# First feed-forward projection of a two-block transformer kernel, with the weights stationary in TensorE and the 256 tokens moving

## The reference, cut to what matters

```python
h = _rmsnorm(x, g_pre_ffn[l]) * (1.0 + sc2) + sh2
f = jnp.square(jax.nn.relu(h @ w_ff1[l])) @ w_ff2[l]
x = x + gt2 * _rmsnorm(f, g_post_ffn[l])
```

## Time and profile before

| | |
|---|---|
| median of 3 runs | 1873.92 us |
| runs | 1872.31 to 1875.08 us |
| span of the profiled execution, first to last instruction | 1870.4 us |
| device time of the profiled execution | not listed apart from the span; the median lies 3.5 us above the span |
| PE busy, share of the span | 1826.9 us, 98% |
| weight loads (PEld) busy | 1495.8 us, 80% |
| DVE busy | 1297.3 us, 69% |
| ACT busy | 901.1 us, 48% |

### The profile page before, as it was taken

The page is one execution under the profiler, slowest core; times in us unless marked ns, Lnnn a source line. Parts: engine busy times, 40 slices in busy tenths (PEclk is TensorE's granted clock), DMA queues, the critical chain, the costliest instruction groups (busy, mean ns, idle before and its releaser), DMA issues.

```text
span 1870.4 us, 25828 instructions
## 1 busy us (share of the span) xinstructions
PE 1826.9 (98%) x8418; PEld 1495.8 (80%) x8418; DVE 1297.3 (69%) x1700; ACT 901.1 (48%) x1272; POOL 181.8 (10%) x268
## 2 busy tenths in 40 slices
PE   8999999989999999999999998999999999999998
PEld 6777777778688888888888886888888888888886
DVE  5777787885798677686776888666666664545545
ACT  6555565453444544544444455444444444444443
POOL 1212211210000000031000130000000010000000
PEclk9999999989999999999999999999999999999999
DMA  7767776836486686688888874877777755555553
GB/s 253 259 223 250 231 237 227 282 117 213 129 266 220 200 277 212 215 302 284 279 281 283 300 260 147 259 231 236 229 233 229 236 195 194 192 193 193 195 192 136
DMA packets 180029, 424.90 MB, mean 227 GB/s; under 512 B 15376, under 2 KB 15616, under 8 KB 179584
## 3 DMA queue, kind: packets, MB, share of 16 engines
q1 hardware_dynamic: 151376, 320.07, 52.0%
q0 software_dynamic: 28304, 103.89, 17.7%
q10 hardware_dynamic: 288, 0.16, 0.1%
HBM read 421.97 MB, written 2.10 MB: 227 GB/s over the span
## 4 chain that ended last, share of the span: by engine, by line
PE 84%; DVE 7%; DMA 5%; issue 3%; ACT 2%; DVEq 0%; POOL 0%; ACTq 0%; POOLq 0%
PE bank L1723 26%; PE bank L1725 26%; PE bank L1724 26%; DMA ada_raw<-in_w_ada 4%; DVE w_lo L1086 2%; PE bank L1779 2%; DVE acc_a L1096 1%; PE bank L1853 1%; PE bank L1852 1%; DVE acc_b L1096 1%; PE bank L1871 1%; DVE y L1224 1%; DMA raw<-in_w_in_a 0%; PE bank L1863 0%; DVE y L1254 0%
## 5 line engine op out<-in xcount | busy, mean ns | idle before, releaser
L1086 DVE TENSOR_TENSOR w_lo<-raw,w_hi 128x1024 fp32r<-128x1024 f32 (+1 forms) x608 | 741.7, 1225 | 420.8 <-ACT w_hi L609 419.5
L609 ACT ACTIVATE w_hi<-raw 128x1024 fp32r<-128x1024 f32 (+1 forms) x608 | 637.0, 1050 | 743.9 <-PE bank L1725 684.2
L1723 PE MATMUL bank<-w_hi,h_hi 128*128 128x512 f32 (+1 forms) x2304 | 910.4, 395 | 11.5 <-DVE h_lo L1187 5.4
L1725 PE MATMUL bank<-w_hi,h_lo 128*128 128x512 f32 (+1 forms) x2304 | 898.4, 390 | 0.0
L1724 PE MATMUL bank<-w_lo,h_hi 128*128 128x512 f32 (+1 forms) x2304 | 897.2, 389 | 0.0
L1723 PEld LDWEIGHTS bank<-w_hi,h_hi 128*128 128x128 f32 x2304 | 434.8, 189 | 105.1 <-DVE w_lo L1086 6.0
L1725 PEld LDWEIGHTS bank<-w_hi,h_lo 128*128 128x128 f32 x2304 | 434.6, 189 | 91.6
L1724 PEld LDWEIGHTS bank<-w_lo,h_hi 128*128 128x128 f32 x2304 | 435.2, 189 | 85.9
L508 POOL DMA_DIRECT2D ada_raw<-in_w_ada x192 | 103.0, 537 | 1123.7 <-DVE acc_a L1096 867.0
L1096 DVE SCALAR_TENSOR_TENSOR acc_a<-ada_raw,cond,acc_a 128x1024 f32<-128x1024 f32 x128 | 164.4, 1284 | 31.2 <-DMA ada_raw<-in_w_ada 30.9
L1096 DVE SCALAR_TENSOR_TENSOR acc_b<-ada_raw,cond,acc_b 128x1024 f32<-128x1024 f32 x64 | 85.3, 1333 | 12.1 <-DMA ada_raw<-in_w_ada 12.0
(11 more groups left out here) (183 smaller groups left out, 1028.3 us busy)
## 6 DMA issues: line engine op xcount, KB each, us to landing
raw<-in_w_ff SPq DMA_DIRECT2D x256, 512.0 KB, 4.4
ada_raw<-in_w_ada POOLq DMA_DIRECT2D x192, 512.0 KB, 4.8
raw<-in_w_in SPq DMA_DIRECT2D x176, 512.0 KB, 4.5
raw<-in_w_in_a SPq DMA_DIRECT2D x72, 512.0 KB, 4.6
raw<-in_w_out_a SPq DMA_DIRECT2D x32, 512.0 KB, 4.7
raw<-in_w_o SPq DMA_DIRECT2D x32, 512.0 KB, 4.7
raw<-in_w_moba SPq DMA_DIRECT2D x16, 512.0 KB, 4.6
raw<-in_w_dsa SPq DMA_DIRECT2D x16, 512.0 KB, 4.8
```

The costliest lines, as they stand in the source:

```text
L609: act.activation(used(w_hi, turn, s), used(raw, turn, s), ACT.Copy).then_inc(hi_ready, 1)
L1086: dve.tensor_tensor(used(w_lo, turn, s), used(raw, turn, s), used(w_hi, turn, s).bitcast(F32), ALU.subtract).then_inc(lo_ready, 1)
L1723: pe.matmul(out_ap, hi, rhs_hi, start=start, stop=False)
L1725: return pe.matmul(out_ap, lo, rhs_hi, start=False, stop=stop)
```

## The change

The projection's matmuls swap their operands. A 128x128 tile of the weights (`w_hi` or `w_lo`) is stationary, and all 256 tokens of a slice of `h_hi` or `h_lo` move. A unit becomes 24 matmuls of 256 columns (2 banks, 2 slices, 2 halves of a bank, 3 products). A PSUM bank now holds two groups of 128 features by 256 tokens side by side. The result has the layout of `f_t`, so DVE's square writes `f_t` itself, and the transposes, their two copies and the semaphores `f_turned` and `f_t_ready` go. ACT's relu waits for the squares of the turn before. `f_tok` is called `f_pos`.

On ScalarE:

```diff
-            def relu(p, c, turn):
-                for t in range(T):
-                    chunk_result(t, turn, c + CHUNK_FF1)
-                    act.wait_ge(f_turned, c * T + t + 1)
-                    act.activation(f_tok[:, t, :], pair[p][t][:, :], ACT.Relu).then_inc(evicted[p][t], 1)
-            def keep_f(c):
-                act.wait_ge(f_turned, c * T + 1 + T)
-                act.activation(f_t[:, bass.ds(c * 4, 4), 0:P], two(banks[TURNED][:, :], 4), ACT.Copy)\
-                    .then_inc(f_t_ready[0], 1)
+            def relu(p, c, turn, first=False):
+                for b in range(T):
+                    chunk_result(b, turn, c + CHUNK_FF1)
+                    if not first:
+                        act.wait_ge(f_sq, c * T + b + 1 - T)
+                    act.activation(f_pos[:, b, :], pair[p][b][:, :], ACT.Relu).then_inc(evicted[p][b], 1)
             def ff1_turn(c):
                 for s in range(UPT):
                     split(c + TURN_FF1, s + AHEAD)
-                    if s == 4:
-                        keep_f(c - 1)
```

On VectorE:

```diff
-            def square(p, use):
-                for t in range(T):
-                    dve.wait_ge(evicted[p][t], use + 1)
-                    dve.tensor_tensor(f_tok[:, t, :], f_tok[:, t, :], f_tok[:, t, :], ALU.mult).then_inc(f_sq, 1)
-            def keep_f(c):
-                dve.wait_ge(f_turned, c * T + 2 + T)
-                dve.tensor_copy(f_t[:, bass.ds(c * 4, 4), P:SEQ], two(banks[OUTS][:, :], 4)).then_inc(f_t_ready[1], 1)
+            def square(p, c, use):
+                for b in range(T):
+                    dve.wait_ge(evicted[p][b], use + 1)
+                    dve.tensor_tensor(f_t[:, bass.ds(c * 4 + 2 * b, 2), :], two(f_pos[:, b, :]), two(f_pos[:, b, :]),
+                                      ALU.mult).then_inc(f_sq, 1)
```

On TensorE:

```diff
-            def turn_f(c):
-                for t in range(T):
-                    pe.wait_ge(f_sq, c * T + t + 1)
-                    turn_rows(f_tok, t, 4, banks[TURNED + t], f_turned)
+            def ff1_unit(turn, s, p, use, h=None):
+                if h is not None:
+                    pe.wait_ge(h_lo_ready, h + s + 1)
+                pe.wait_ge(lo_ready, unit_of(turn, s) + 1)
+                for b in range(T):
+                    if s == 0:
+                        pe.wait_ge(evicted[p][b], use)
+                    for kk in range(KG):
+                        k = KG * s + kk
+                        for half in range(2):
+                            at = kk * CH + (2 * b + half) * P
+                            out_f = pair[p][b][:, half * SEQ:(half + 1) * SEQ]
+                            hi, lo = w_hi[:, s % SLOTS, at:at + P], w_lo[:, s % SLOTS, at:at + P]
+                            pe.matmul(out_f, hi, h_hi[:, k, :], start=s == 0 and kk == 0 and half == 0, stop=False)
+                            pe.matmul(out_f, hi, h_lo[:, k, :], start=False, stop=False)
+                            mm = pe.matmul(out_f, lo, h_hi[:, k, :], start=False,
+                                           stop=s == UPT - 1 and kk == KG - 1 and half == 1)
+                    if s == UPT - 1 and b == 0:
+                        mm.then_inc(front_done, 1)
+                mm.then_inc(mm_done, 1)
             def ff1_turn(c, p, use):
                 for s in range(UPT):
-                    chunk_unit(c + TURN_FF1, s, p, use)
-                    if s == 3:
-                        turn_f(c - 1)
+                    ff1_unit(c + TURN_FF1, s, p, use)
...
-            norm_turn(2, TURN_FF1, PAIR_A, 23, H_NORM2)
+            norm_turn(2, TURN_FF1, PAIR_A, 23, H_NORM2, ff1_unit)
...
             ff2_half(1, 0, 0, start=True)
-            turn_f(15)
             pe.wait_ge(gain_ready, 8)
             ff2_half(0, 1, 0, start=True).then_inc(mm_done, 1)
-            for t in range(T):
-                pe.wait_ge(f_t_ready[t], D_FF // CH)
             ff2_half(1, 1, 0, start=True).then_inc(mm_done, 1)
             ff2_turn(0, 0, 2)
             ff2_turn(1, 1)
```

More of the change, by code:

```diff
@@ L234, in two_block_kernel @@
             f_t = sb("f_t", [P, D_FF // P, SEQ], on=a)
-        f_tok = acc_b[:, 0:T * CH].rearrange("p (t n) -> p t n", t=T)
+        f_pos = acc_b[:, 0:T * CH].rearrange("p (t n) -> p t n", t=T)
         norm_tmp = post_gain[:, 0:2 * KG * SEQ].rearrange("p (b n) -> p b n", b=2)
@@ L352, in two_block_kernel @@
         f_sq = sem("f_sq")
-        f_turned = sem("f_turned")
-        f_t_ready = [sem(f"f_t_ready{t}") for t in range(T)]
         f_hi_ready = sem("f_hi_ready")
@@ L1017, in ff1_turn @@
                     split(c + TURN_FF1, s + AHEAD)
-                    if s == 4:
-                        keep_f(c - 1)
             norm_turn(2, TURN_FF1)
-            relu(PAIR_A, 0, TURN_FF1)
+            relu(PAIR_A, 0, TURN_FF1, first=True)
             with act.Fori(0, 7) as it:
@@ L1054, in ff2_turn @@
                         round_f(c + 1, 1 - b)
-            split(TURN_FF2, AHEAD)
-            keep_f(15)
-            for t in range(T):
-                act.wait_ge(f_t_ready[t], D_FF // CH)
-            for s in range(1, UPT):
+            for s in range(UPT):
                 split(TURN_FF2, s + AHEAD)
                 if s == 4:
+                    act.wait_ge(f_sq, D_FF // CH * T)
                     round_f(1, 1)
@@ L1073, in _ @@
                 act.wait_ge(y_squared, 4 * CHUNKS + n + 1)
-                act.activation(f_tok[:, 0, :], banks[t * CHUNKS + c][:, :], ACT.Square, accum_out=y_sq[:, t, c:c + 1])\
+                act.activation(f_pos[:, 0, :], banks[t * CHUNKS + c][:, :], ACT.Square, accum_out=y_sq[:, t, c:c + 1])\
                     .then_inc(y_squared, 1)
@@ L1638, in _ @@
             residual_turn(2, TURN_FF1 - 1, PAIR_B, (23, 25), y2)
-            def square(p, use):
-                for t in range(T):
-                    dve.wait_ge(evicted[p][t], use + 1)
-                    dve.tensor_tensor(f_tok[:, t, :], f_tok[:, t, :], f_tok[:, t, :], ALU.mult).then_inc(f_sq, 1)
-            def keep_f(c):
-                dve.wait_ge(f_turned, c * T + 2 + T)
-                dve.tensor_copy(f_t[:, bass.ds(c * 4, 4), P:SEQ], two(banks[OUTS][:, :], 4)).then_inc(f_t_ready[1], 1)
+            def square(p, c, use):
[3 more added lines that the diff above has]
+                                      ALU.mult).then_inc(f_sq, 1)
             norm_turn(2, TURN_FF1, pre_gain)
-            square(PAIR_A, 23)
+            square(PAIR_A, 0, 23)
             dve.wait_ge(acc_init[5], 16)
@@ L1663, in _ @@
                             ada(it * 4 + 160, n, acc_a, it * 2 + b)
-                    square(1 - b, it + 25 - b)
+                    square(1 - b, it * 2 + 1 + b, it + 25 - b)
             def low_f(c, b):
@@ L1681, in _ @@
             gate_gain(1, 2, SCORES)
-            square(PAIR_B, 32)
+            square(PAIR_B, 15, 32)
             gate_gain(1, 3, SCORES + 1)
@@ L1797, in norm_turned, with norm_turn @@
                 ins.then_inc(n_turned, 1)
-            def norm_turn(r, turn, p, use, h):
+            def norm_turn(r, turn, p, use, h, unit_of_turn=chunk_unit):
                 ahead = 4 if r else 3
@@ L1810, in norm_turn @@
                 for s in range(UPT):
-                    chunk_unit(turn, s, p, use, h)
+                    unit_of_turn(turn, s, p, use, h)
                     if s + ahead < UPT:
@@ L1821, in rows @@
                     .then_inc(mod_rows, 1)
-            for credit in (og_turned, y_turned, f_turned):
+            for credit in (og_turned, y_turned):
                 pe.sem_inc(credit, T)
@@ L2074, in _ @@
             for s in range(UPT):
-                chunk_unit(TURN_FF2 - 1, s, PAIR_B, 32)
-                if s == 3:
-                    turn_f(14)
+                ff1_unit(TURN_FF2 - 1, s, PAIR_B, 32)
                 if s >= 5:
```

10 lines of the change are left out of this document (1 added, 9 removed).

## The result

| | before | after |
|---|---|---|
| median, first comparison (7 runs each) | 1873.92 us | 1879.9 us |
| ratio after / before, 95% interval | | 1.003, 1.002 to 1.004 |
| span of the profiled execution | 1870.4 us | 1872.7 us |
| one projection turn, mean of turns 45 to 58 | 22.67 us | 23.04 us |

The account below looks back on a forecast made before the run. The prediction took PE's queue of matmuls to bound the projection. Span 1870.4 - 14.7 (transposes) + 2.1 (matmuls) = 1857.8 us; with the median 3.5 us above the span, the forecast was 1861.3 us, range 1857 to 1876 us.

Parts of the forecast that it names:

- What bounds the stage: First feed-forward projection: PE never waits within turns, so the stage lasts exactly as long as PE's queue of matmuls.
- The transposes, -14.7 us: 16 sets of eight transposes on PE, 0.92 us each, disappear: 14.7 us less.
- The matmuls, +2.1 us: Projection: 192 matmuls of 256 columns at 114 ns replace 96 of 512; 0.13 us more per turn, 2.1 us in all.
- in the middle by the columns: Projection matmul spacing read from 80-column and 512-column matmuls: 0.442 ns a column, so 113.5 ns at 256 columns.
- rival A: Projection: 13.4 ns fixed cost per matmul, so 120 ns each, 5.8 us slower in all, 1879.7 us; chance 0.13.
- Rival B: Projection: weight tiles as stationary operand slow the stream beside them; 117 ns spacing, gain only 3.5 us; chance 0.18.
- rival D: Projection: stationary loads not hidden, 188 ns a matmul, 215 us more, about 2089 us; chance 0.03 together with anything unthought of.
- rival C: Projection: columns cost less, loads pace the matmuls at 110 ns; 25 us less, 1849 us; chance 0.04.
- theory 1: Set up for the experiments: float32r matmul distance is N/2.4 + 13.3 ns at any size, unless loads set it; 120.0 at 256.
- The first turn: Projection's first turn, partly at the low clock: counted like the others, 0.13 us more for its matmuls.
- The start of the second projection: Without its transposes PE reaches the gain wait at 1515.16 us, product just in time; if late, costs at most 0.92 us.
- ACT and DVE: Projection: their copies per turn, 0.58 and 0.68 us, go; neither held PE up, so worth nothing.

Follow-up runs that it names:

- experiment 1: Matmuls alone in cells of 24, computation left out, float32r by column count: 226.5 ns apart at 512 columns, 119.8 at 256, 111.1 at 224.
- experiment 6: Matmuls alone, other types and orders: bf16 189.4 ns at 448 columns; also one-512-column-matmul-for-both-halves kernel, grouped in fours: 1872.85 us, ratio 0.9992.
- experiments 1 and 2: The second of these: kernel before, transposes and operands kept, each 512-column projection matmul split into two of 256: 1892.82 us, ratio 1.0086.
- experiment 7: Kernel with one 512-column matmul for both activation halves, now grouped in eights: 1874.05 us, ratio 0.9995; last turn done likewise too: 1874.79 us, 1.0002.

## Why the prediction was wrong, step by step

- **What bounds the stage**: right. PE has no wait in the 14 turns before or after, and the turn after is 192 distances of 120.0 ns, 23.04 us.
- **The transposes, -14.7 us**: right. Leaving them out alone gave 0.91 us a turn in the traces and 14.3 us by the ratio (11.3 to 17.4).
- **The matmuls, +2.1 us**: the step that failed, and it is the size of one term, the distance of 114 ns taken "in the middle by the columns". It is 120.0 ns. Between the kernel without transposes and the changed one the 14 turns alone take 322.56 - 304.64 = 17.9 us more; the forecast gave 1.8 us to them. The mechanism was named (a fixed 13.4 ns a matmul) and stood as the upper bound and as rival A with 0.13.
- **Where the reading went wrong.** It rested on the first 80-column matmul: its successor 0.03 us later and its duration of 199 ns. These are one reading and not two, since the duration is the distance (35 ns) and 164. And it is the single matmul at a change of pattern. Its value was no accident: in the six cells of experiment 1 with 64 to 224 columns the second matmul starts 28, 46, 57, 72, 85 and 100 ns behind the first, 1 to 7 ns above N/2.4. But from the second on these cells stand near 111.7 ns, so the first distance is not the price of a steady one, and at 256 columns even the first is 118 ns. The attention rows were no support for float32r either. Their durations, 0.38 us at 256 columns of plain float32, are those of a 512-column bf16 matmul in experiment 6 (379 ns), whose fixed part is 2.5 ns, so they gave the price of another type. The one even, repeated figure of the same type was 226.7 - 213.3 = 13.4.
- **Rival B**, interference by the place of the tile: shown wrong for this change (experiments 1 and 2), though the 6.7 ns for a shifted tile at 512 columns are real. At 256 columns the shifted cell was 1.6 ns faster than the aligned one.
- **Loads**: rival D did not occur, and rival C's pace of 110 to 112 ns is seen from 240 columns down, where the loads set it. The load is busy through the whole 14 turns after the change (322.56 of 322.56 us), yet the turn is the same 120.0 x 192 that theory 1 gives. The Trainium skill ("Perfetto Trace Analysis", section on the most-contended engine) would take this busy share as a sign that no headroom is left. At 224 columns the loads step by 111.7 ns with a duration of 192, so there was room of 8 ns a matmul even at full busy share.
- **The first turn**: the prediction counted it like the others. The trace has +0.25 us, but the 1.28 us of its matmuls and the clock are mixed in this (see the balance). **The start of the second projection**: from the last sum of the gate to the last matmul 348.11 us became 347.38, a gain of 0.73 of the 0.92, and no new wait for the gain.
- **ACT and DVE**: right, their time was worth nothing. It was not so in experiment 7, where work of ACT, POOL and DVE at the end of the stage was late.

The Trainium skill ("TensorE: Matmul & The Clock Gate", section "Back-to-back issue gap") has N/2.4 + 2.5 ns for an isolated matmul. Experiment 6 finds this within 0.3 ns for bf16, and 11 ns more for float32r.

**Open:** whether the 13.3 ns of float32r belong to the stream or to the load beside it. Every matmul here had both operands of one type, so no run parts them, and the cells with fewer stationary columns changed the distance at 256 columns but not at 384. The first distances of the small cells, 1 to 7 ns above N/2.4, say that a float32r stream doesn't always pay the 13.3. Why 512 and 256 columns in turn cost 6.6 ns a pair, and 384 and 256 nothing, is also only measured, not explained.

## What to carry to other kernels

Before splitting matmuls, subtract N/2.4 from the steady start-to-start distance of the same type: what is left is paid once per matmul as long as tiles and pattern stay the same, here 13.3 ns for float32r and 2.5 for bf16, so that halving 1536 matmuls cost more than the 128 transposes they saved. Price an operation by an even row of many, of the same type, and never by the one at a change of pattern; and don't count a modelled duration as a second witness of a distance. Where a change has one unmeasured price, work out the price at which its sign turns (118.1 ns here), and if the upper bound lies beyond it, let that case weigh.

## What the runs showed of the hardware that was not expected

- Float32r, new stationary tile each time, clock at 1.00: 226.7 ns at 512 columns, 120.0 at 256, and a floor of 111.7 from 240 columns down. At the head of experiment 1, behind 13 us in which PE was idle, the 512-column matmuls start 427 ns apart until 16.6 us, which is 512 columns at 1.2 GHz with nothing on top. The view by stretches shows 1.00 there, but the records of the clock in this trace begin only at 16.73 us, so that the 1.00 ahead of them is no measurement. In turn 44 of the changed kernel, where the granted clock is 0.50, the 256-column ones start 213 ns apart, again with nothing on top.
- Bf16, the same: 215.8 ns at 512, 55.8 at 128, 29.1 at 64; its load lasts 98 ns against 188.
- The shift of either operand by 32 bytes costs 6.7 ns at 512 columns and is a gain of 1.6 (stationary) or 3.3 ns (moving) at 256. At 384 it costs 3.4 for the moving operand and nothing for the stationary one.
- Alternating 512 and 256 columns costs 353.3 ns a pair instead of 346.7, and behind matmuls of 256 columns it takes five of 512 until they stand at 227 ns again. Alternating 384 and 256 costs nothing (293 ns).
